# Loading four rounds of cached keys and the samples' columns one stage early in a fused decoder layer

## What is computed

```python
h = x + 0.5 * rms_norm(swiglu_ffn(rms_norm(x, norms[0]), f1_gu, f1_d), norms[1])
u = rms_norm(h, norms[2]); proj = u @ w_in
# group A: 4 heads, gated delta rule over chunks (short conv on q/k/v, decay gates g and beta)
# group B: 8 heads, stick-breaking attention
z = q.k / sqrt(64) + bias;  a = sigmoid(z) * prod_{s<j<t} (1 - sigmoid(z_j));  o = a @ v
h = h + rms_norm(concat(A, B) @ w_o, norms[3])
y = h + 0.5 * rms_norm(swiglu_ffn(rms_norm(h, norms[4]), f2_gu, f2_d), norms[5])
```

## Time and profile before

| | |
|---|---|
| three executions | 2354.01, 2358.11, 2359.06 us (median 2358.11) |
| the profiled execution | 2357.36 us, its span 2355.7 us |
| mean granted TensorE clock | 0.986 |
| busy share of the span | PE 95%, DVE 70%, ACT 45%, POOL 2% |
| moved by DMA | 345.27 MB, mean 147 GB/s |
| stage a ends, stage b begins | 1209.2 us, 1214.4 us |
| stage b ends, stage c begins | 1501.7 us, 1503.1 us |

### The profile page before, as it was taken

One profiled execution on the slowest core, in us unless ns is written; L12 is line 12 of the kernel. 1 busy time (PEld: TensorE's weight loads), 2 busy tenths in 40 slices (PEclk: granted clock), 3 DMA queues, 4 the chain that ended last, 5 costly groups with the idle time before them and its releaser, 6 DMA issues. The chain is left out here.

```text
span 2355.7 us, 47025 instructions
## 1 busy us (share of the span) xinstructions
PE 2247.7 (95%) x18388; PEld 1994.2 (85%) x18388; DVE 1642.4 (70%) x2790; ACT 1054.0 (45%) x1919; POOL 48.9 (2%) x108
## 2 busy tenths in 40 slices
PE   7999999999999999999958899899999999999998
PEld 7999999987879888888856766578999999997786
DVE  7766766656886488676657987657676766665886
ACT  7322222234554576566645665435522222233453
POOL 0000000000000100000010001010000000000000
PEclk9999999999999999999979999999999999999999
DMA  5343333365464445344448978723143333436454
GB/s 161 103 136 119 103 133 102 116 215 183 134 184 136 114 100 111 88 101 95 86 112 312 309 269 291 237 78 119 56 159 106 124 122 93 145 123 229 138 168 152
DMA packets 391360, 345.27 MB, mean 147 GB/s; under 512 B 106249, under 2 KB 299145, under 8 KB 391200
## 3 DMA queue, kind: packets, MB, share of 16 engines
q1 hardware_dynamic: 391200, 343.08, 47.1%
HBM read 271.54 MB, written 88.25 MB: 153 GB/s over the span
## 5 line engine op out<-in xcount | busy, mean ns | idle before, releaser
L1242 PE MATMUL a_q<-a_uh,a_p_hi 128*128 128x352 f32 x672 | 234.1, 348 | 0.7 <-ACT a_xp L1333 0.6
L1244 PE MATMUL a_q<-a_uh,a_p_lo 128*128 128x352 f32 x672 | 217.1, 323 | 0.0
L1243 PE MATMUL a_q<-a_ul,a_p_hi 128*128 128x352 f32 x672 | 216.5, 322 | 0.0
L1242 PEld LDWEIGHTS a_q<-a_uh,a_p_hi 128*128 128x128 f32 x672 | 126.9, 189 | 23.7 <-issue 21.6
L1243 PEld LDWEIGHTS a_q<-a_ul,a_p_hi 128*128 128x128 f32 x672 | 127.6, 190 | 0.1
L1244 PEld LDWEIGHTS a_q<-a_uh,a_p_lo 128*128 128x128 f32 x672 | 126.6, 188 | 0.0
L884 PE MATMUL c_q<-c_b_hi,c_a_hi 128*128 128x512 f32 x264 | 104.8, 397 | 3.1 <-DVE c_a_lo L783 2.0
L884 PE MATMUL a_q<-a_b_hi,a_a_hi 128*128 128x512 f32 x264 | 104.3, 395 | 3.0 <-DVE a_a_lo L783 2.9
L885 PE MATMUL c_q<-c_b_hi,c_a_lo 128*128 128x512 f32 x264 | 104.1, 394 | 0.0
L886 PE MATMUL c_q<-c_b_lo,c_a_hi 128*128 128x512 f32 x264 | 103.9, 393 | 0.0
L885 PE MATMUL a_q<-a_b_hi,a_a_lo 128*128 128x512 f32 x264 | 103.4, 392 | 0.0
(11 more groups left out here) (738 smaller groups left out, 7608.5 us busy)
## 6 DMA issues: line engine op xcount, KB each, us to landing
b_page<-in_cache_v SPq DMA_DIRECT2D x128, 256.0 KB, 4.3
a_w_raw<-in_ffn_gu SPq DMA_DIRECT2D x44, 512.0 KB, 5.2
c_w_raw<-in_ffn_gu SPq DMA_DIRECT2D x44, 512.0 KB, 5.0
a_a_raw<-hid_rows SPq DMA_DIRECT2D x66, 256.0 KB, 2.7
c_a_raw<-hid_rows SPq DMA_DIRECT2D x66, 256.0 KB, 2.7
k_blocks<-in_cache_k SPq DMA_DIRECT2D x64, 256.0 KB, 3.8
b_page<-in_cache_k SPq DMA_DIRECT2D x64, 256.0 KB, 4.3
b_page<-k_blocks SPq DMA_DIRECT2D x64, 256.0 KB, 5.4
```

Of the source, the lines that this page charges most:

```text
L1242: nc.tensor.matmul(self.pm[at % 2][:, 0:TB], wh, self.uh[t][:, c], start=(c == 0), stop=False)
L1243: nc.tensor.matmul(self.pm[at % 2][:, 0:TB], wh, self.ul[t][:, c], start=False, stop=False)
L1244: mm = nc.tensor.matmul(self.pm[at % 2][:, 0:TB], wl, self.uh[t][:, c], start=False, stop=(c == KC - 1))
```

## The change

- `first_half` gets a new stream on SP, `next_stage`. At the end of the projection it loads the samples' columns (one DMA from a new tensor `qk_cols`, already in the layouts of `qs`, `qs_b`, `ks`, `ks_b`) and the four pages of key rounds 0 to 3, into buffers that the projection no longer uses. All 17 DMAs count on one semaphore, `early_in`; whoever needs any of them waits for all.
- `store_columns` writes each tile to `qk_cols` with 5 DMAs (1 and 4 by blocks of 32 rows), where it had 1. There are 8 tiles. All count on one semaphore.
- `key_blocks` is paced closer (13.0 for 14.6), so that it is done earlier.
- Stage b allocates its tiles around the preloaded ones (`Room`). Its SP stream starts with 8 loads, those of the gates first.
- POOL makes the masks for `own` and `sample` last, `qb` is cleared by DVE. Of the copies into `qb`, DVE keeps 16 and ACT gets 16; those of the second group come later in the order. The masks' turns use bank D0 and are split in two.
- Two key rounds stand ahead of the gates; the other key rounds and all value rounds get times lower by 4.1.

```diff
+            def next_stage():
+                yield 446.0
+                sp.wait_ge(attend.E("z_mm"), attend.tiles_done(2))
+                sp.wait_ge(project.E("cols_out"), 640)
+                sp.dma_start(early_cols[:], project.qk_cols).then_inc(early_in, 16)
+                sp.wait_ge(E("blocks"), 16 + 32 * (N_B // 4 * page_table.shape[1]))
+                for n in range(len(PAGE_SLOTS)):
+                    if n == 0:
+                        sp.wait_ge(project.E("rest"), N_UNITS)
+                    elif n == 1:
+                        sp.wait_ge(project.E("blocked"), NAT_UNITS.index(unit_of("conv", 11)) + 1)
+                    elif n == 2:
+                        yield unit_end(N_UNITS - 1) + 1.0
+                        sp.wait_ge(project.E("mm"), piece(N_UNITS - 1, 2) + 1)
+                    numbers = page_numbers(nc, table, 0, n, cache_k.shape[0])
+                    for b in range(4):
+                        if b % 2 == 1:
+                            sp.dma_start(early_page[n][:, b], k_blocks[2 * n + b // 2]).then_inc(early_in, 16)
+                        else:
+                            sp.dma_start(early_page[n][:, b:b + 1, :], cache_k[bass.ds(numbers[b], 1)].rearrange("g p n -> p g n")).then_inc(early_in, 16)
...
-                sp.dma_start(dram[hp], ring[hp % 2][:, T_P:T]).then_inc(self.E(f"cols_out{hp % 2}"), 16)
+                sp.dma_start(self.qk_cols[:, 2 * m, hp, :], ring[hp % 2][:, T_P:T]).then_inc(self.E("cols_out"), 16)
+                for c in range(P // BLOCK):
+                    sp.dma_start(self.qk_cols[BLOCK * hp:BLOCK * hp + BLOCK, 2 * m + 1, c, :],
+                                 ring[hp % 2][BLOCK * c:BLOCK * c + BLOCK, T_P:T]).then_inc(self.E("cols_out"), 16)
...
-                    yield 12.0 + 14.6 * n
+                    yield 12.0 + 13.0 * n
...
-KEY_AT = (-16.12, 1.821, 10, 1.461)
-VALUE_AT = (41.05, 1.723, 17, 2.126)
+KEY_AT = (-20.22, 1.821, 10, 1.461)
+QUERY_AT = (-62.0, 2.0)
+MASKS_AT = -9.0
+FIRST_KEYS = (-60.0, -58.2)
+VALUE_AT = (36.95, 1.723, 17, 2.126)
...
+            n = ROUNDS * gi + p
+            return FIRST_KEYS[n] if n < len(FIRST_KEYS) else paced(KEY_AT, n)
...
-                for n in range(2 * len(KEY_ROUNDS)):
+                for n in range(SLOTS, 2 * len(KEY_ROUNDS)):
...
+            def query_blocks():
+                act.wait_ge(early_in, EARLY_IN)
...
+                        step = nc.scalar.activation(qb[k, gi, pair, :, to].rearrange("p c (b o) q -> p c b o q", o=2)[:, :, :, 1], src[:, :, :, 1], ACT.Copy)
...
+            nc.vector.memset(qb[:], 0.0).then_inc(E("qb_zero"), 1)
```

More of the change, by code:

```diff
@@ L97, in at, with __init__, sb @@
         return self.nc.alloc_sbuf_tensor_at(f"{self.tag}_{name}", shape, dt, offset=at)
+class Room:
+    def __init__(self, nc, tag, start, end, taken):
+        self.nc, self.tag, self.free = nc, tag, []
+        for at, size in sorted(taken):
+            self.free.append([start, at])
+            start = at + size
+        self.free.append([start, end])
+    def at(self, name, offset, shape, dt=F32):
+        return self.nc.alloc_sbuf_tensor_at(f"{self.tag}_{name}", shape, dt, offset=offset)
+    def sb(self, name, shape, dt=F32):
+        size = -(-4 * math.prod(shape[1:]) // 32) * 32
+        for span in self.free:
+            at = -(-span[0] // 32) * 32
+            if at + size <= span[1]:
+                span[0] = at + size
+                return self.at(name, at, shape, dt)
+        raise ValueError(name)
 def new_cols(i):
@@ L1190, in store_columns @@
         for hp in range(H_SB // 2):
[L1191 removed]
+            for m, (kind, ring) in enumerate((("query", self.q), ("key", self.k))):
                 n = unit_of(kind, hp)
@@ L2444, in delta_and_sample @@
-        rest, u = s.sb("rest", [P, H, P]), s.sb("u", [P, H, P])
-        state = [s.sb(f"state{z}", [P, H, P]) for z in range(2)]
+        end = tail_at + MIX_TAIL
+        room = Room(nc, "b3", nc.sbuf_base, end, [(tail_at + o, 4 * 4 * SB) for o in PAGE_SLOTS] + [(tail_at + COLS_AT, 4 * 4 * 4 * T_S)])
+        s.sb("fence", [P, (end - nc.sbuf_base) // 4])
+        page = early_page
+        qs, qs_b, ks, ks_b = (early_cols[:, n] for n in range(4))
+        table = room.sb("table", [1, PAGES * N_B], I32)
@@ new lines, in delta_and_sample @@
+        v_new = room.sb("v_new", [T_S, SB])
+        k_turned = [room.sb("k_turned", [P, 4, 4, P])[:], w_early[:].rearrange("p r (b c n) -> p (r b) c n", b=2, n=P)]
+        ex = room.sb("ex", [P, G, KEYS])
+        run = room.sb("run", [P, KEYS])
+        qb = room.sb("qb", [P, G, 4, 4, R])
+        bias = room.sb("bias", [H_SB, 1])
+        row_bias = room.sb("row_bias", [P, 1])
+        pick_t = room.sb("pick_t", [H_SB, P])
+        own_t, sample_t = room.sb("own_t", [T_S, G, P]), room.sb("sample_t", [T_S, G, P])
@@ new lines, in delta_and_sample @@
+        pick, own, sample = room.sb("pick", [P, H_SB]), room.sb("own", [P, G, T_S]), room.sb("sample", [P, G, T_S])
+        zeros = room.sb("zeros", [P, 1])
+        wt = room.sb("wt", [P, 2, P])
+        o_rows = room.sb("o_rows", [P, G, SB])
+        stage = o_rows
+        abx = room.sb("abx", [P, NT + 1, 8])
+        dt, a_log = room.sb("dt", [P, 4]), room.sb("a_log", [P, 4])
+        gx, ge, gw, gwi, gl, last = (room.sb(n, [P, NT + 1, 4]) for n in "gx ge gw gwi gl last".split())
+        norm, rn = room.sb("norm", [P, NT + 1, 8]), room.sb("rn", [P, NT + 1, 8])
@@ new lines, in delta_and_sample @@
+        newton = room.sb("newton", [P, 8])
+        gm = room.sb("gm", [T_S, N_B, 4])
+        rows = [room.sb(f"rows{z}", [P, QKV]) for z in range(3)]
+        sc = room.sb("sc", [P, 2, H, P])
+        dec = room.sb("dec", [P, H, P])[:]
+        mt = [room.sb(f"mt{z}", [P, H, P]) for z in range(2)]
+        squares = sc[:].rearrange("p z h c -> p (z h c)")
+        kn_t = [room.sb(f"kn_t{z}", [P, H, P]) for z in range(2)]
+        qn_t = room.sb("qn_t", [P, H, P])
+        qe_t = [room.sb(f"qe_t{z}", [P, H, P]) for z in range(2)]
@@ new lines, in delta_and_sample @@
+        p5 = p1
+        squares_h, gate = room.sb("squares_h", [P, D]), room.sb("gate", [P, DN])
+        g_dn, g_sb = room.sb("g_dn", [P, P]), room.sb("g_sb", [P, DH])
+        mean_h, root_h, newton_h = (room.sb(n, [P, H_DN + H_SB]) for n in ("mean_h", "root_h", "newton_h"))
+        x_half = room.sb("x_half", [2 * R, H, 2 * R])
+        inverse = [room.sb(f"inverse{z}", [P, H, P]) for z in range(2)]
+        rest, u = room.sb("rest", [P, H, P]), room.sb("u", [P, H, P])
+        state = [room.sb(f"state{z}", [P, H, P]) for z in range(2)]
@@ L3246, in _ @@
[L3246 to L3253 removed]
+            interleave(queries(), masks_of_samples(), chain(), advance(), gates(), norms(), prepare(), key_copies(), logits(), weigh(), keep(), finish())
```

223 lines of the change are left out of this document (105 added, 118 removed).

## The result

| | before | the change |
|---|---|---|
| median | 2357.02 us (9 runs, 2352.56 to 2359.06) | 2366.24 us (9 runs, 2359.65 to 2372.72) |
| ratio | 1 | 1.0046, 95% interval 1.0031 to 1.0060 |
| profiled execution, its span | 2357.36, 2355.7 us | 2366.24, 2364.5 us |

The change is slower by about 0.46%, some 11 us. The forecast, 2351.4 us, was on the other side, and the time lies outside its range.

A forecast was written before the change was run, and what follows sets the result against it. Stage b: late gates at the start, then saturated DMA, PE and DVE nearly full, PE as bound, and a closing chunk chain. Terms -2.5 - 4.3 + 0.5 - 4 + 4.3 = -6.0 gave 2351.4 us, range 2344 to 2359.

The forecast's parts named there:

- Term 1: Stage b's start: the gates start earlier than 1227.79 us, worth -2.5 us (bounds -1.0 to -4.5).
- Term 2: Stage b's dense stretch: two key rounds move to PE's idle start, -4.3 us; masks and copies moving in, +0.5.
- Term 3: Stage b's dense stretch: four rounds' transfers move to stage a, worth -4 us (bounds 0 to -10.0).
- the first rival, DMA-bound: DMAs bind stage b's dense stretch, so the transfers save 10 us: sum -12.0, 2345.4 us; chance 0.17.
- Term 4: Stage b's end gets longer, +4.3 us: +1.5 for the chain, +2.6 for two page rounds, 0.2 for hops.
- the first sign of being wrong: Stage b: the prediction is wrong if its start is early but the middle gains nothing.
- No change: Stage b: DVE and the chunk chain bind, so two rounds fewer on PE save 0.8: -1.5, 2355.9 us; chance 0.24.
- The slower rival, SP's queue: Projection: 32 more store issues delay weights, up to +17.2 us, 2368.6; chance 0.11 together with an end at its upper bound.
- the right side: Whole kernel: the change is slower by over 0.2%; chance 0.12.

The follow-up runs named there:

- e15: The change itself, unaltered, timed again beside two variants on one chip: 1.0050 of the kernel before, 2365.43 us.
- e7: e1 with the gates first and the two early key rounds between the gates' sums and chunk 0: 0.9963 of the kernel before, 2348.95 us.
- e8: e1 with no key round ahead of the gates, loads still early: 0.9953 of the kernel before, 2343.28 us; repeats 0.9956 and 0.9969.
- e1: The change with key rounds, value rounds and weighing at the old places: 0.9985 of the kernel before, 2352.34 us; repeat 0.9990.
- e9: e8 with the 16 page loads of rounds 0 to 3 issued at stage b's start instead of in stage a: 1.0002 of the kernel before, 2354.10 us.
- e3: The change with only the weighing moved back by 4.1 to its old places, rounds still early: 1.0010 of the kernel before, 2359.73 us.
- e5: The kernel before with only the second group's weighing 4.1 earlier: 1.0028 of the kernel before, 2363.39 us.
- e10: e8 with each of the columns' 32 block stores split in two, so 32 more issues on SP: 0.9974 of the kernel before, 2349.90 us.
- e6: The change with values and weighing at their old places, only the key rounds early: 0.9995 of the kernel before, 2356.60 us.
- e11: e8 with the first group's weighing 2.0 later: 0.9960 of the kernel before, 2344.71 us.

## Why the prediction was wrong

- *Term 1, the gates, -2.5:* right in size. They start 3.5 us sooner after the stage's start (9.85 us for 13.34), with the first score round at 1.83 us and the second at 1.05, so between the warm and the cold sum; in the repeat (e15) 2.2 us sooner (11.10), with both at the lower clock. One reading in it was off: half of 3.37 us is no cold turning of eight, which takes 1.94 to 1.97 us.
- *Term 2, two rounds "now run where PE was idle: -4.3":* failed. PE was idle there, but the rounds' copies and logits stand in front of the gates on DVE. e7 and e8 put the gates first, and their sums come 6.5 us sooner than in e1, where PE then waits behind chunk 0's rows. e1 against e8 makes the two rounds a cost of 4 to 7.5 us. I compared with the gates' start of before, 13.3 us late, and not with where they could have started.
- *Term 3, the transfers, -4:* too small, and in the wrong place. In e8's order the pages' early loading is worth some 10 us (e9), as the first rival's sum had it, but not in the dense stretch: it lets PE turn pages and reach chunk 0 from the start. In the dense stretch the waits named for pages did not go, though I had forecast it; they fell from 3.0 to 2.0 us (0.68 and 1.32). What the early pages are worth in the change's own order no run shows.
- *Term 4, the end, +4.3:* its first part is confirmed: +1.6 for +1.5 and 0.2 more. The +2.6 of the two value rounds can't be told apart from what comes next.
- **The step that failed most: I read the shift by 4.1 as an order of rounds and priced only its two ends.** What is between has no term of its own in the sum: I took it as less work, -7.7 us by chunk 7's u. Measured from the stage's start it is +7.6. That the start is early and the middle gains nothing was the first sign of being wrong that I had named. The weighing's times hang on the key rounds', and this is most of it: 8.5 us by e3, and 6.6 us in the kernel before by e5. It was to be seen ahead: ACT's new order at chunk 3 has a step of the weighing in front of a copy for which PE waits, in a stretch where I had named PE the bound.
- *Rivals:* DMA-bound had the size of the early pages (e9) right, and their place wrong. "No change" had the reason nearest to what happened, the chunk chain, without its price. The slower rival, SP's queue, was the wrong mechanism: stage a ends no later. In the fourteen profiles of kernels with the change's stores in stage a (e10, with more, not counted) stage b starts at 1210.4 to 1216.4 us, with a median of 1212.9, and in the two with the old stores at 1214.45 and 1214.03. The stores' issues took 422 ns by blocks and 631 (queries) or 389 ns (keys) whole, in the median; SP still stood 177.6 us waiting for the attention's rows between 750 and 1190 us. I gave the right side 0.12.

What stays open: how the rest of the change's loss (e3 to e1, some 6 us) divides between keys and values. By the ratios it is 3.5 us for the values (e3 to e6) and 2.4 for the keys (e6 to e1), neither clear of the intervals. Open is also by which of its steps the weighing costs: the wait at chunk 3 is one place, and PE's idle time fell by 7.0 us in e3. Moving the weighing to other places than those of before was tried once (e11), without gain.

## What to carry to other kernels

Where an order is made of times, a shift of one table moves everything that is computed from it. List those pieces, and look for the long instructions among them on engines that serve short dependent chains; here one set of long steps, a 1.9 us instruction ahead of a 0.4 us copy among them, cost 6.6 to 8.5 us, more than the 4.3 us that the two rounds were to bring. When an engine is idle at a stage's start, first ask what the others are waiting for: filling the gap paid here only behind that work (e7 and e8 against e1). And test the parts of a combined change apart: here the early pages were worth some 10 us, and the new order lost 17 to 22 (e8 against the change).

## What the runs showed that I had not expected

Short waits cost more than their length here, by the granted clock. Behind the wait of 2.60 us a value round took 1.94 us instead of 1.06; behind the 0.47 us wait at the same place in the kernel before it took 1.06. From 1400 to 1430 us the mean clock was 0.94 before and 0.83 in the change (stretches of the kernel before, then of the change):

```profile
1400.00:1430.00 30.00, 27.13 (x473) 17.32 (x466) 25.20 (x71) 16.97 (x48) 2.08 (x4) 0.94 0.92 327
```

```profile
1400.00:1430.00 30.00, 24.76 (x374) 15.88 (x374) 19.86 (x54) 13.27 (x35) 1.96 (x4) 0.83 0.85 292
```

Waits also don't simply vanish: e11 removed one of 3.66 us, and three came up that sum to 6.2.

On the clock at the stage's start the runs don't agree with each other. In the change's profile the two score rounds behind the first transposes took 1.83 and 1.05 us, in its repeat (e15), with the same instructions, 1.94 and 1.93. The row of the kernel before on which I had relied, 16 transposes in 3.37 us and a warm score round behind them, did not repeat either. In e5, where PE's order there is the same, it reads:

```profile
1232.75 3.67 PE L2763 MATMUL b_S<-w_ident,b_page 128*128 128x128 f32 x16
1236.35 1.94 PE L2775 MATMUL b_S<-b_k_turned,b_qb 128*32 128x128 f32 x32
```

So to set the Trainium skill's rule (TensorE: Matmul & The Clock Gate, PE-mode transpose: they don't count for the full clock) aside on that row was thin. These runs neither show the rule nor refute it.
